# Reordering the opening of a one-core hybrid layer: unread products first, memory rows scaled on ScalarE, weight parts moved ahead

## The reference, cut to what matters

```python
h = _rmsnorm(x, norm_mix_g)                        # x: 256 tokens x 1024
p = h @ w_in                                       # columns: q k | v | r | a | u | sv | two gates
log_a   = log_sigmoid(a_low @ w_a2 + b_a) / 16     # gated linear attention, chunks of 64 tokens
cum     = cumsum(log_a)                            # within a chunk
q_in, k_in, k_out = q*dk**-0.5*exp(cum), k*exp(-cum), k*exp(cum_last - cum)
y_a = rmsnorm(gla(q_in, k_in, k_out, v)) * silu(r) @ w_proj_a
y_b = (gelu(u) * (tril(sgu_w) @ layernorm(gelu(sv)) + b)) @ w_proj_b
x   = x + (sigmoid(g_a)*y_a + sigmoid(g_b)*y_b) @ w_mix_out
mem_n = _rmsnorm(mem, norm_mem_g)                  # 256 memory rows x 1024
x   = x + cross_attention(_rmsnorm(x), mem_n)
x   = x + moe(_rmsnorm(x))                         # 32 experts, top 4, 12 MB of weights each
out = _rmsnorm(x, norm_final_g)
```

## Time and profile before

| | us |
|---|---|
| median of 3 runs | 1233.13 (1232.56 to 1233.39) |
| the profiled execution | 1231.48 |
| its span in the trace | 1229.4 |
| PE busy in the span | 1162.0 (95%) |
| DVE, ACT, POOL busy | 334.4, 279.8, 204.2 |
| moved by DMA | 453.29 MB, mean 369 GB/s |

### The profile page before, as it was taken

One profiled execution on the slowest core, in us unless ns is written; L12 is line 12 of the kernel. 1 busy time (PEld: TensorE's weight loads), 2 busy tenths in 40 slices (PEclk: granted clock), 3 DMA queues, 4 the chain that ended last, 5 costly groups with the idle time before them and its releaser, 6 DMA issues.

```text
span 1229.4 us, 13747 instructions
## 1 busy us (share of the span) xinstructions
PE 1162.0 (95%) x5582; PEld 542.6 (44%) x5582; DVE 334.4 (27%) x663; ACT 279.8 (23%) x401; POOL 204.2 (17%) x64
## 2 busy tenths in 40 slices
PE   6999999999999999999999999999999999999996
PEld 6788898986333333333333333333333333333332
DVE  2643283034122222222222222222222222222222
ACT  5554445453111111121111111111211111111112
POOL 7876777830000000000000000000000000000000
PEclk9999999999999999999999999999999999999999
DMA  9654656658999999999999999999999999999994
GB/s 318 204 171 138 190 171 210 220 226 339 426 394 428 427 428 427 429 427 429 429 429 427 428 429 429 429 427 427 431 428 428 427 430 429 428 428 429 430 428 181
DMA packets 53946, 453.29 MB, mean 369 GB/s; under 512 B 6326, under 2 KB 6908, under 8 KB 29340
## 3 DMA queue, kind: packets, MB, share of 16 engines
q1 hardware_dynamic: 53840, 452.85, 89.6%
q10 hardware_dynamic: 76, 0.02, 0.0%
HBM read 451.81 MB, written 1.05 MB: 368 GB/s over the span
## 4 chain that ended last, share of the span: by engine, by line
PE 73%; DMA 13%; DVE 8%; issue 2%; ACT 2%; SPq 1%; POOL 1%; DVEq 0%; ACTq 0%
PE ps L1671 30%; PE ps L1707 16%; PE ps L1274 12%; DMA late<-in_w_e 9%; PE ps L1648 4%; DMA raw<-in_w_e 3%; PE ps L1318 3%; DVE shared L1222 2%; DVE shared L1219 2%; DVE shared L1216 2%; PE ps L1696 2%; PE ps L1474 1%; PE ps L1657 1%; DVE shared L1217 1%; ACT shared L756 1%
## 5 line engine op out<-in xcount | busy, mean ns | idle before, releaser
L1671 PE MATMUL ps<-late,shared 128*64 128x512 f32 x1200 | 268.0, 596 | 4.7 <-DMA late<-in_w_e 4.5
L454 POOL TENSOR_TENSOR pairs<-raw,pairs 128x2048 fp32r<-128x2048 f32 x42 | 196.5, 4689 | 73.3 <-ACT pairs L533 73.2
L1192 DVE TENSOR_TENSOR rows<-ps,rows 128x512 f32<-128x512 f32 x128 | 79.6, 684 | 413.8 <-PE ps L1648 413.8
L1671 PEld LDWEIGHTS ps<-late,shared 128*64 128x64 f32 x1200 | 82.7, 137 | 176.5 <-issue 165.4
L750 ACT ACTIVATE shared<-shared 128x512 f32<-128x512 f32 x32 | 20.1, 629 | 540.8 <-DVE shared L1216 540.8
L1274 PE MATMUL ps<-pairs,hT 128*128 128x512 f32 x576 | 134.1, 392 | 2.0 <-POOL pairs L454 2.0
L1274 PEld LDWEIGHTS ps<-pairs,hT 128*128 128x128 f32 x576 | 107.3, 188 | 25.5 <-POOL pairs L454 2.7
L1671 PE MATMUL ps<-raw,shared 128*64 128x512 f32 x496 | 112.9, 597 | 1.8 <-DMA raw<-in_w_e 1.8
L1707 PE MATMUL ps<-late,shared 128*64 128x512 f32 x496 | 110.5, 594 | 2.5 <-ACT shared L756 2.5
L1216 DVE TENSOR_SCALAR shared<-ps 128x512 f32<-128x512 f32 x32 | 22.1, 692 | 292.9 <-PE ps L1671 292.9
L533 ACT ACTIVATE pairs<-raw 128x2048 fp32r<-128x2048 f32 x42 | 80.2, 1916 | 63.1 <-PE ps L1274 35.4
(11 more groups left out here) (216 smaller groups left out, 961.8 us busy)
## 6 DMA issues: line engine op xcount, KB each, us to landing
late<-in_w_e SPq DMA_DIRECT2D x106, 2048.0 KB, 27.7
raw<-in_w_e SPq DMA_DIRECT2D x42, 2048.0 KB, 26.7
extra<-in_w_e SPq DMA_DIRECT2D x22, 2048.0 KB, 25.9
shared<-in_w_e SPq DMA_DIRECT2D x22, 2048.0 KB, 27.4
raw<-in_w_in SPq DMA_DIRECT2D x18, 1024.0 KB, 5.5
raw<-in_w_xk SPq DMA_DIRECT2D x4, 1024.0 KB, 5.4
raw<-in_w_mix_out SPq DMA_DIRECT2D x4, 1024.0 KB, 4.9
raw<-in_w_xv SPq DMA_DIRECT2D x4, 1024.0 KB, 5.1
```

The lines of the kernel that those rows point to most:

```text
L454: g.tensor_tensor(low, raw_half(m), high, ALU.subtract).then_inc(s["low_made"], 1)
L1192: V.tensor_tensor(rows[:, t, c], ps[:, SCATTER_BANKS[k], :], rows[:, t, c], ALU.add).then_inc(s[f"y_added{k}"], 1)
L1671: last = M.matmul(ps[64 * j:64 * j + 64, HIDDEN_BANKS[h], :], xeT[:, c % 2 * W1_SUB + part, j0:j0 + SLOTS], w[:, h * D + j * HALF:h * D + ...
```

## The change: what it does

- PE, which waited for the small vectors first, now multiplies the unit matrix by itself 20 times into the bank of q; nothing reads the result. The small vectors are turned after x's first group (xT00) instead of ahead of it.
- DVE takes the reciprocal and makes the diagonal before it copies the small vectors out.
- ACT makes the first half of r's high part ahead of the decay's Abs, Exp and Ln. It scales the memory rows (two instructions of 1024 columns) after the second half of r, which DVE did before in four instructions of 512. It copies v out and makes the two halves of sv ahead of the two exponentials of cum, and the first half of u ahead of the exponential of cum_diff.
- DVE makes cum_diff after the keys instead of ahead of q_in.
- POOL masks w_sgu just ahead of the low part of u's first half (the ninth) instead of the third.
- PE's wait for the memory rows counts tiles (t + 1) where it counted half tiles.

```diff
+FIRST_IDLE_PRODUCTS = 20
             low_part(1)
-            pool.wait_ge(s["wsgu_in"], 16)
-            g.affine_select(out=w_sgu, in_=w_sgu, ...).then_inc(s["wsgu_masked"], 1)
             for m in range(2, HALVES):
+                if m == 2 * PIECES.index("u"):
+                    pool.wait_ge(s["wsgu_in"], 16)
+                    g.affine_select(out=w_sgu, in_=w_sgu, ...).then_inc(s["wsgu_masked"], 1)
                 low_part(m)
...
-            high_parts("v", 1)
+            high_parts("r", 0)
...
             high_parts("r", 1)
+            sc.wait_ge(s["mem_rstd"], 1)
+            for t in range(TT):
+                A.activation(side[:, t, :], side[:, t, :], ACT.Copy,
+                             scale=stat[:, N_MEM + 4 + t:N_MEM + 5 + t]).then_inc(s["mem_normed"], 1)
+            copy_out("v0", values[:, 0, :])
+            copy_out("v1", values[:, 1, :])
+            high_parts("sv", 1)
             sc.wait_ge(s["cum_made"], 2)
             A.activation(ec, cum, ACT.Exp, scale=1.0 / TAU).then_inc(s["cum_exp"], 1)
             A.activation(z, cum, ACT.Exp, scale=-1.0 / TAU).then_inc(s["cum_neg_exp"], 1)
+            high_parts("u", 0)
             sc.wait_ge(s["cum_diff"], 1)
             A.activation(lns, lns, ACT.Exp, scale=1.0 / TAU).then_inc(s["rest_exp"], 1)
-            copy_out("v0", values[:, 0, :])
-            copy_out("v1", values[:, 1, :])
-            high_parts("sv", 1)
...
-            filled(ve, "vecs")
-            V.tensor_copy(vecs[:], bank("vecs")[:, 0:38]).then_inc(...)
             inv(N_X + 4, 2, "x_std", "x_rstd")
...                                                # the diagonal
+            filled(ve, "vecs")
+            V.tensor_copy(vecs[:], bank("vecs")[:, 0:38]).then_inc(...)
...
             inv(N_MEM + 4, 2, "mem_std", "mem_rstd")
-            scale_rows(side, side, N_MEM + 4, "mem_rstd", "mem_normed")
...                                                # logarithms, scans
-            V.tensor_tensor(lns..., cum4[:, :, GLA_C - 1:GLA_C].to_broadcast(...), cum4,
-                            ALU.subtract).then_inc(s["cum_diff"], 1)
...                                                # q_in, keys
+            V.tensor_tensor(lns..., cum4[:, :, GLA_C - 1:GLA_C].to_broadcast(...), cum4,
+                            ALU.subtract).then_inc(s["cum_diff"], 1)
...
             pe.wait_ge(s["ident_made"], 2)
-            pe.wait_ge(s["small_in"], 16 * 6)
-            transposes("vecs", [(vec_rows[:], P)])
+            for _ in range(FIRST_IDLE_PRODUCTS):
+                M.matmul(bank("q")[:, 0:P], ident[:], ident[:], start=True, stop=True, skip_group_check=True)
...                                                # one group of x turned
+                    if k + t == 0:
+                        pe.wait_ge(s["small_in"], 16 * 6)
+                        transposes("vecs", [(vec_rows[:], P)])
...
-                rows_T("memT", t, k, side, "mem_normed", 2 * t + k + 1)
+                rows_T("memT", t, k, side, "mem_normed", t + 1)
```

More of the change, by code:

```diff
@@ L478, in _ @@
             low_part(1)
-            pool.wait_ge(s["wsgu_in"], 16)
-            g.affine_select(out=w_sgu, in_=w_sgu, compare_op=ALU.is_ge, fill=0.0, base=0,
-                            pattern=[[0, SGU_G], [-1, P]], channel_multiplier=1).then_inc(s["wsgu_masked"], 1)
             for m in range(2, HALVES):
+                if m == 2 * PIECES.index("u"):
+                    pool.wait_ge(s["wsgu_in"], 16)
+                    g.affine_select(out=w_sgu, in_=w_sgu, compare_op=ALU.is_ge, fill=0.0, base=0,
+                                    pattern=[[0, SGU_G], [-1, P]], channel_multiplier=1).then_inc(s["wsgu_masked"], 1)
                 low_part(m)
@@ L802, in norm_tile @@
                     ins.then_inc(s[done], 1)
[L804 to L810, removed]
             def copy_out(group, dst):
@@ L847, in _ @@
                                    stat[:, N_X + 5:N_X + 6]).then_inc(s["x_sq"], 1)
-            filled(ve, "vecs")
-            V.tensor_copy(vecs[:], bank("vecs")[:, 0:38]).then_inc(bank_emptied[bank_of("vecs")], 1)
             inv(N_X + 4, 2, "x_std", "x_rstd")
@@ L855, in _ @@
                     s["diag_made"], 1)
+            filled(ve, "vecs")
+            V.tensor_copy(vecs[:], bank("vecs")[:, 0:38]).then_inc(bank_emptied[bank_of("vecs")], 1)
             emptied(ve, "vecs")
@@ L883, in _ @@
             cum4 = cum.rearrange("p f (n c) -> p (f n) c", c=GLA_C)
-            V.tensor_tensor(lns.rearrange("p f (n c) -> p (f n) c", c=GLA_C),
-                            cum4[:, :, GLA_C - 1:GLA_C].to_broadcast([P, 2 * NCH, GLA_C]), cum4,
-                            ALU.subtract).then_inc(s["cum_diff"], 1)
             filled(ve, "q")
@@ L897, in _ @@
                                 ALU.mult).then_inc(s["keys_made"], 1)
+            V.tensor_tensor(lns.rearrange("p f (n c) -> p (f n) c", c=GLA_C),
+                            cum4[:, :, GLA_C - 1:GLA_C].to_broadcast([P, 2 * NCH, GLA_C]), cum4,
+                            ALU.subtract).then_inc(s["cum_diff"], 1)
             ve.wait_ge(s["rest_exp"], 1)
```

## The result

The changed kernel takes 1224.71 us (median of 5 runs, 1223.28 to 1225.05) against 1233.13 (median of 5, 1229.45 to 1238.01): ratio 0.9941, interval 0.9924 to 0.9958, so 5.2 to 9.4 us faster. The forecast was 1228.1, in a range from 1227.0 to 1231.8. The direction was right, the size outside the range.

The account below looks back on a forecast made before the run. The end was set by when PE's r products start the DMA-bound expert stream; 2.5 us from the opening plus 2.5 from two waits for POOL gave 1233.13 - 5.0 = 1228.1 us, range 1227.0 to 1231.8.

Parts of the forecast that it names:

- Unread products end at 8.4: At PE's start, the 20 unit-matrix products were to end at 8.4 us, with bounds of 6.0 and 10.4.
- qk at 12.2: After x is turned at the fast pace, PE's qk products were to start at 12.2 us instead of 14.70.
- v's first low part at 25.3: POOL, no longer masking w_sgu first, was to finish v's first low part at 25.3 us instead of 29.2.
- v at 25.55: PE was to reach the first v product at 25.55 us, 0.25 after POOL, so without the 0.95 us wait.
- r at 37.8: PE's first r product was to start at 37.8 us instead of 42.80, without the 1.06 us wait for POOL.
- The upper bound for DVE: Logarithms and both scans on DVE each wait for one POOL low part; last scan ends 47.15, q_in read by 49.2.
- The rival at q's bank: Scans, exponentials and q_in queue behind POOL, emptying q's bank too late for sv: 1235.3 us, chance 0.07.
- the expert stage: DMA-bound from 296 to 1190 us at 427 GB/s without a pause; taken as unchanged in length, only starting earlier.
- the median's distance from the profiled execution: Whole-kernel median taken as 1.65 us above the profiled execution, before and after the change.
- PE's wait for POOL is 2.0 us in two parts: Between 25 and 45 us PE waits 0.95 us ahead of v and 1.06 ahead of r; both were to vanish.
- the memory rows on ACT: Scaling in ACT's gap at 34.3 to 36.4 us, 2 x 1.06 us; claimed to put nothing on the path.
- 1.3 us to r's high part: ACT making it at 27.7 to 29.6 us removes PE's 1.06 us wait ahead of r and its 0.25 lost overlap.

Follow-up runs that it names:

- the second trace: The kernel before, unchanged, timed and profiled again: 1233.00 us, ratio 1.0005.
- one pair of kernels: Changed kernel with 43 unread products, 1230.56 us, against the same with the 32-row output biases replaced by unread 128-row products, 1229.33 us.
- the repeat: The changed kernel, unedited, timed again beside the kernel before: 1224.98 us, ratio 0.9945.
- the four groups: The fourteen follow-up kernels were timed in four groups, each beside the kernel before, whose median there was between 1230.7 and 1232.4 us.
- the opening alone: Kernel before with only 20 unread products on PE and the reciprocal and diagonal ahead of the small vectors: 1232.15 us, ratio 1.0008.

## Why the prediction was right in direction and too small

*What held, by its own steps.* Unread products end at 8.4 (the next starts at 8.36); qk at 12.2 (12.42); v's first low part at 25.3 (25.4); v at 25.55 (25.88); no wait ahead of r, and r at 37.8 (about 38.0); the dense stage 5.0 us shorter (4.9). The upper bound for DVE was the right end: each of the three operations waited for one low part, the last scan ended at 47.4 (forecast 47.15), and q_in was read by 48.9 (49.2). The rival at q's bank did not occur. The Trainium skill (SBUF — State Buffer, Who interferes with whom) says that a VectorE instruction with two SBUF inputs contends with a GpSimd instruction that reads SBUF; the trace agrees, with 4.58 and 9.96 us for 0.69 and 1.27 us of work beside POOL's low parts.

*By how much it missed.* 1228.1 - 1224.7 = 3.4 us. The profiled execution was to be 1226.5 and is 1224.3, which is 2.2 of it: 1.9 are the expert stage, 0.3 lie outside the span. The other 1.2 are the median's distance from the profiled execution, 1.65 before and 0.41 after.

*The step that failed* is that distance, taken over unchanged ("The median of the runs is 1.65 above the profiled execution, so 1233.13 - 5.0"), and beneath it the term "PE's wait for POOL is 2.0 us in two parts", of which v's part was put at 0.95 us. The 0.95 came from one execution, in which w_sgu landed at 24.01. In the four other traces in which the mask and the load stand where they stood before, the mask started at 24.52, 24.86, 25.17 and 26.20, and where nothing filled PE's time the wait was 3.8 to 4.6 us; in two of these three a faster opening lengthened it. In the kernel before itself the second trace has 3.81. After such a wait the clock was at its lower level while v ran, which cost 1.4 to 1.5 us more. So what the change removes is, in the median, more than what it removes from that one trace: moving the mask alone brings r forward by 0.75 us against that trace, and the median by 2.6 to 3.1. The forecast knew that POOL waited for this transfer; it asked what the wait costs in the trace, and not how much it varies and what a wait of 4 us does to PE behind it.

*The other part* is the expert stage, which the forecast left as long as it was because a mean over 894 us showed DMA "without a pause"; the windows above have 131 GB/s in one stretch of 2.5 us. In ten traces without a fall of the clock near 337 the stage is 897.5 to 898.7 us (mean 898.2); in the three with a fall of 3.4 us it is 898.8, 898.8 and 899.8, in the three with 6.8 us 900.2 to 901.1. The profiled execution of before had one of 3.4, that of after none. Of the 1.9 us between them about 1.0 goes with such a fall, by these means, and the rest is within the spread of the ten. That the 32-row output biases have a part in it is supported by one pair of kernels. Why it comes in few runs of the changed kernel (one of six in the repeat, by the mean clock) and in all ten of those with 43 unread products stays open.

*Put together:* 4.9 us by the start of r, against the luckiest of the five openings with w_sgu in its old place. What the medians have beyond it, 3.5 us in the first measurement and 1.0 in the repeat (1230.91 - 1224.98 = 5.9; by the ratio 6.8 and so 1.9), is put down to openings of before that are worse than the profiled one, and to falls. The first measurement's 1233.13 for the kernel before is itself high: in the four groups it was 1230.7 to 1232.4. The fastest runs of before (1228.8 to 1229.5) are 5.0 to 6.2 us above the fastest of the changed kernel (1223.3 and 1223.8), nearer to the 4.9. How the rest divides between openings and falls was not measured.

*A part that was costed at nothing* was not nothing: the memory rows on ACT. By itself it lies off the path, but r's early high part closes the gap of POOL in which DVE had scaled them; left on DVE, with the opening of before, it costs 2.7 us (4.3 by the ratios). The exponentials' new place is worth 2.7 us in the changed kernel (3.0 by the ratios, whose intervals just overlap). Neither changes the sum for the whole, in which all parts are present, but the forecast had credited 1.3 us to r's high part as if it could stand alone.

The unread products are worth 2.0 us in the changed kernel (intervals overlap; the first expert product comes 1.8 to 2.1 us sooner with them) and the mask's place 6.9; with the mask in its old place the rest of the change gives nothing that can be measured (1.0003). The parts therefore don't add up: the mask alone gives 2.6 to 3.1 us, the opening alone nothing, and the opening behind the moved mask another 2.3 to 3.1. No run beat the changed kernel.

## What to carry to other kernels

A wait that ends with a transfer should be read in more than one execution before it is priced: here 0.95 us in one was 3.8 in the next, and moving the mask alone lowered the median by 2.6 us, where the first trace had promised 0.75. An in-order engine that serves a chain should not hold, in front of it, work that waits for a late transfer, even if the work is 0.6 us long. And closing one engine's gap takes away the room in which another engine's operations ran: before filling a gap of GpSimd, list what VectorE does in it.

## What the runs showed of the hardware

After waits of PE of 3.8 to 4.6 us at v and of 2.0 to 2.3 us at sv the granted clock read 0.50 in a following stretch of 2.5 us; after waits of 0.9 to 1.1 us it did not, and unread products in the place of a wait of this kind kept it at 1.00. It also fell in six traces while PE was busy all the time, at the end of or right behind eight records that used 32 rows; ten traces, nine of them with the same eight records, had no fall there. Four scaling instructions of DVE (fp32, one SBUF input) took 9.45 us beside POOL's low parts for 1.67 in a gap of POOL; instructions with two SBUF inputs were held in the same way, while q_in, with one input in PSUM, kept its 0.69 us. A transfer of 256 KB with the same transfers ahead of it landed between 24.01 and 26.20 us in two executions of one program.
